# A hybrid attention layer on one core: new homes for the rotary tables, the dilated mask, the far values and the probability tiles

## The reference

```
h = x @ w_in + b_in                      # 1024 x 3072: qa ka va | qb kb vb | qc | z
oa = banded attention, window 128, 8 query heads on 2 key heads, rotary, learned sinks
ob = dilated attention, 4 heads, rotary: key distances <= 128 (step 1), <= 512 (step 4),
     <= 2048 (step 16), merged by their softmax denominators
oc = attention of 4 heads to keys and values from mem @ w_mem
y  = concat(rms(oa), rms(ob), rms(oc)) * g_branch * silu(z)
x  = layer_norm(2 ** 0.25 * x + y @ w_out)
```

## Time and profile before

| what | value |
|---|---|
| median of three runs | 519.87 us |
| span of the profiled execution, first to last instruction | 512.1 us |
| the profiled execution's own time from outside | not listed; the median lies 7.8 us above the span |
| PE (TensorE matmul) busy | 487.5 us, 95% |
| DVE / ACT / POOL busy | 328.4 / 214.9 / 72.7 us |
| mean granted TensorE clock | 0.992 |

### The profile page before, as it was taken

How to read it: one execution, slowest core, us unless ns; L and a number is a source line. 1 busy time by engine, 2 the same in 40 slices (tenths; PEclk the granted TensorE clock), 3 DMA queues, 4 the chain that set the end, 5 groups by cost and what they waited for, 6 DMA issues and landing times.

```text
span 512.1 us, 9694 instructions
## 1 busy us (share of the span) xinstructions
PE 487.5 (95%) x3480; PEld 443.9 (87%) x3480; DVE 328.4 (64%) x908; ACT 214.9 (42%) x488; POOL 72.7 (14%) x53
## 2 busy tenths in 40 slices
PE   4999999999999979999999898999989999999993
PEld 4999999999999968888888787898878788888882
DVE  4776645557666723444444568878797969798734
ACT  5632222021212035555463659655444454444530
POOL 0000000000000000111101101023232323231425
PEclk9999999999999989999999999999999999999998
DMA  8955472647622453321322179324232414241022
GB/s 288 375 194 146 126 236 82 206 140 257 217 89 93 142 147 105 102 86 56 107 85 91 54 234 316 99 63 135 71 127 60 149 53 148 63 142 48 1 83 82
DMA packets 51710, 67.83 MB, mean 132 GB/s; under 512 B 9552, under 2 KB 41296, under 8 KB 51664
## 3 DMA queue, kind: packets, MB, share of 16 engines
q1 hardware_dynamic: 51088, 66.17, 40.4%
q10 hardware_dynamic: 576, 1.05, 0.6%
HBM read 51.18 MB, written 16.02 MB: 131 GB/s over the span
## 4 chain that ended last, share of the span: by engine, by line
PE 88%; DVE 7%; ACT 2%; DMA 1%; issue 1%; POOLq 0%; POOL 0%; SPq 0%; ACTq 0%; DVEq 0%
PE long_ps L948 15%; PE o_ps L907 9%; PE wide L770 8%; PE wide L772 7%; PE wide L771 7%; PE long_ps L849 5%; PE long_ps L847 5%; PE long_ps L848 5%; PE narrow L887 4%; PE wide L875 4%; PE wide L876 3%; PE wide L781 2%; PE wide L782 2%; PE wide L783 2%; PE narrow L925 1%; DVE nb L1349 1%
## 5 line engine op out<-in xcount | busy, mean ns | idle before, releaser
L770 PE MATMUL wide<-x_hi,w_hi 128*128 128x256 f32 x320 | 88.5, 277 | 0.2
L771 PE MATMUL wide<-x_lo,w_hi 128*128 128x256 f32 x320 | 88.3, 276 | 0.0
L772 PE MATMUL wide<-x_hi,w_lo 128*128 128x256 f32 x320 | 88.3, 276 | 0.0
L770 PEld LDWEIGHTS wide<-x_hi,w_hi 128*128 128x128 f32 x320 | 60.1, 188 | 0.5 <-issue 0.5
L771 PEld LDWEIGHTS wide<-x_lo,w_hi 128*128 128x128 f32 x320 | 60.1, 188 | 0.0
L772 PEld LDWEIGHTS wide<-x_hi,w_lo 128*128 128x128 f32 x320 | 60.1, 188 | 0.0
L1029 ACT ACTIVATE spill<-turn 128x512 fp32r<-128x512 f32 x21 | 13.3, 633 | 99.3 <-DVE turn L1261 73.2
L948 PE MATMUL long_ps<-wo_hi,y_hi 128*128 128x512 f32 x128 | 53.1, 415 | 0.0
L1510 POOL TENSOR_TENSOR g_lo<-g_raw,g_hi 128x1024 fp32r<-128x1024 f32 x6 | 14.3, 2385 | 273.1 <-ACT g_hi L1034 273.1
L948 PE MATMUL long_ps<-wo_lo,y_hi 128*128 128x512 f32 x128 | 52.3, 408 | 0.0
L948 PE MATMUL long_ps<-wo_hi,y_lo 128*128 128x512 f32 x128 | 51.7, 404 | 0.0
(11 more groups left out here) (154 smaller groups left out, 1208.9 us busy)
## 6 DMA issues: line engine op xcount, KB each, us to landing
q_spill<-spill SPq DMA_DIRECT2D x32, 256.0 KB, 2.5
q_pair<-q_spill SPq DMA_DIRECT2D x128, 64.0 KB, 2.0
w_raw<-in_w_qkv SPq DMA_DIRECT2D x12, 512.0 KB, 5.7
x_raw<-in_x_t SPq DMA_DIRECT2D x16, 256.0 KB, 7.7
g_raw<-in_w_gate SPq DMA_DIRECT2D x8, 512.0 KB, 3.5
q_pair<-q_spill SPq DMA_DIRECT2D x32, 128.0 KB, 2.7
q_pair<-q_spill SPq DMA_DIRECT2D x128, 32.0 KB, 1.8
wo_raw<-in_w_out SPq DMA_DIRECT2D x8, 512.0 KB, 4.7
```

Source lines behind the costliest of these rows:

```text
L770: pe.matmul(dst, w_hi[s][:, k, f], t_hi[:, k, cols], start=(k == 0), stop=False)
L771: pe.matmul(dst, w_hi[s][:, k, f], t_lo[:, k, cols], start=False, stop=False)
L772: mm = pe.matmul(dst, w_lo[s][:, k, f], t_hi[:, k, cols], start=False, stop=(k == KT - 1))
```

## The change

- `cos_t` and `sin_t` now lie in the bytes of `v_far`. Nothing shares with `mask_b` any more.
- `mask_b` is loaded among the first loads, behind `sides`.
- The eight `v_far` loads move from jobs 5 to 8 into SP's attention loop, two in each of v = 6, 7, 8, 9.
- `prob[0]` and `prob[1]` trade bytes (21 turned jobs is odd), so `prob[0]` lies on `spill[1]` and `prob[1]` on `spill[0]`.
- ACT waits ahead of the loop for the store of m = 19 only. DVE waits for no store ahead of the loop; it waits for both at unit 1, its first write into a `prob` tile.

```
+FAR_VALUES_AT = 6
...
-        v_far = at("v_far", [P, 2, CLASSES, HB, VW], F32, Region(nbytes(2, CLASSES, HB, VW)).base)
+        r_v = Region(nbytes(2, CLASSES, HB, VW))
+        v_far = at("v_far", [P, 2, CLASSES, HB, VW], F32, r_v.base)
+        cos_t = at("cos_t", [P, SEQ], F32, r_v.base)
+        sin_t = at("sin_t", [P, SEQ], F32, r_v.base + nbytes(SEQ))
...
-        prob = [at(f"prob{s}", [P, SEQ], F32, r_t.base + s * nbytes(SEQ)) for s in range(2)]
+        n_turned = len(plan.turned)
+        prob = [at(f"prob{s}", [P, SEQ], F32, r_t.base + (n_turned + s) % 2 * nbytes(SEQ)) for s in range(2)]
...
-        cos_t = at("cos_t", [P, SEQ], F32, r_p.base)
...
-        r_m = Region(nbytes(SEQ))
-        mask_b = at("mask_b", [P, SEQ], F32, r_m.base)
-        sin_t = at("sin_t", [P, SEQ], F32, r_m.base)
+        mask_b = at("mask_b", [P, SEQ], F32, Region(nbytes(SEQ)).base)
...
             sp.dma_start(sides[:, :, :], sides_d).then_inc(mask_a_in, 16)
+            sp.dma_start(mask_b[:, :], mask_b_d).then_inc(mask_b_in, 16)
...
-                if 5 <= n < 5 + CLASSES:
-                    load_far_values(n - 5)
...
             sp.wait_ge(h_read, n_jobs)
-            sp.dma_start(mask_b[:, :], mask_b_d).then_inc(mask_b_in, 16)
...
                     load_queries(v + QS - 1)
+                if FAR_VALUES_AT <= v < FAR_VALUES_AT + CLASSES:
+                    load_far_values(v - FAR_VALUES_AT)
...
-            for n in plan.turned[-2:]:
-                act.wait_ge(*spills(n))
+            act.wait_ge(*spills(plan.turned[-2]))
...
                     dve.wait_ge(mask_b_in, 16)
+                    for n in plan.turned[-2:]:
+                        dve.wait_ge(*spills(n))
...
             dve.wait_ge(mask_a_in, 48)
-            for n in plan.turned[-2:]:
-                dve.wait_ge(*spills(n))
```

More of the change, by code:

```diff
@@ L398, in layer @@
         v_c = at("v_c", [P, NBM, HC, VW], F32, Region(nbytes(NBM, HC, VW)).base)
-        v_far = at("v_far", [P, 2, CLASSES, HB, VW], F32, Region(nbytes(2, CLASSES, HB, VW)).base)
+        r_v = Region(nbytes(2, CLASSES, HB, VW))
+        v_far = at("v_far", [P, 2, CLASSES, HB, VW], F32, r_v.base)
+        cos_t = at("cos_t", [P, SEQ], F32, r_v.base)
+        sin_t = at("sin_t", [P, SEQ], F32, r_v.base + nbytes(SEQ))
+        assert r_v.base + nbytes(2, SEQ) <= r_v.end
         r_z = Region(nbytes(FT, SEQ))
```

## The result

Forecast 515.1 us, range 514.3 to 517.2. Measured in the first comparison: **513.44 us** (median of four executions, 510.77 to 513.83) against 519.93 us for the kernel before (four executions, 519.07 to 521.63), a ratio of 0.9864 [0.9834, 0.9894]. The direction was right; the time lies 0.9 us under the range. The ratios leave out executions on record as slow (over 1.5% above the fastest of the same kernel), and in the 5th set these are three of the changed kernel's six, so that 0.9835 rests on three. The two medians of that set, 514.22 and 518.74 us, differ by 0.9%. The kernel before has 90 executions in the later sets of runs, with a median of 519.5 us (514.6 to 523.6); its four of the first comparison have no clock on record and are left out of the 90.

A forecast was written before the change was run, and what follows sets the result against it. TensorE was taken as the bound (88% of the 512.1 us span), so only its idle or slow-clock stretches counted. Terms 3.14 + 1.67 = 4.81 us off 519.87 gave 515.1 us, range 514.3 to 517.2.

The forecast's parts named there:

- Term 1: Start of attention: the wait for the last store moves behind unit 0, so TensorE's transposes begin 3.14 us earlier.
- Term 2: Gate matmuls behind that idle, from 186 us: without the idle the clock does not fall, 1.67 us gained.
- The rule set against this term: Start of attention: very short, frequent idles can swing the clock; then term 2 is 0, sum 3.14 us; rival's chance 0.07.
- The mask as a condition: Unit 1's exponential: with a late mask TensorE would stand over 4 us; early load itself earns 0.
- The far loads and the tables' home at zero: Far loads moved from projection to attention iterations 6 to 9 cost 0; the tables' new home changes no instruction.
- What is late next: At unit 2's scores, 186.2 us: its queries in time by 0.3 to 0.8 us, unit 1's probabilities by 0.4.
- the three runs before spread over 0.9 us: Whole kernel: step that widened the forecast's own range, 514.9 to 515.4, to 514.3 to 516.0 us.
- the median of the runs lies 7.8 us above that span: Whole kernel: the same distance was kept from span to time, giving 519.87 - 4.81 = 515.1 us.
- a span near 507.3 us: Whole kernel: sign that the prediction is right, the span of 512.1 us less 4.81 us.

The follow-up runs named there:

- homes only: Changed kernel with the old probability tiles and store waits put back, keeping new table homes, early mask and moved far loads: 518.40 us, 0.9974 to the kernel before.

## Why the prediction was wrong: its steps and its range

**Term 1, the wait for the store: right.** 3.27 us of idle became 0.10; forecast 0.13. The run without the trade left 2.38 us and cost 2.2 us more than the change. The rest of the span, without the clock's cost, fell by 3.15 us in the 3rd set of runs.

**Term 2, the clock: right on average, wrong in its bounds.** The split of the span into the clock's cost and the rest, over the 90 and the 28 executions, has means of 4.84 and 512.45 us before, 3.15 and 508.97 changed. The clock gave 4.84 − 3.15 = 1.69 us (± 0.4; forecast 1.67) and the rest 3.48 us (± 0.7; 3.0 by the medians, 512.48 − 509.47; forecast 3.14). But 1.67 stood there as an upper bound, read from a single profile, and it is none: behind the same length of idle the loss was 0, 1.6 and 2.7 us, and the fall near 315 us, which the prediction did not know of, comes and goes in both kernels. The earlier trace rows were read as an idle of 1.31 us with a full clock behind it. By the timeline of before that idle is 1.39 us, as the stretch ended just before it did:

```profile
294.08 0.50 PE L822 MATMUL long_ps<-x_hi,g_hi 128*128 128x512 f32 x1 [1.39 <-DVE zt L1342]
```

It is there in all fourteen profiles (1.38 or 1.39 us), each time with a full clock behind. Yet at 314 us a full clock followed an idle of 1.31 us, and a fall one of 1.00. So the row was right for its own place and no rule for another, and one profile cannot carry a bound.

The rule set against this term is from the Trainium skill, page "TensorE: Matmul & The Clock Gate", section "A second HAM failure mode: psum-queue depth-cycling": short but frequent idles between groups of matmuls can make the clock swing as well. At the start of the attention the trace does not show it: 1.00 from 186 to 190 us. At the output weights, where two waits come close together, the trace of the 3rd set of runs fits it (0.94 and 0.72), and three of the five profiles of the changed kernel do not, at 1.00. That fall is in one of two profiles of before and in two of five of the changed kernel, too few to tell whether it has a share in the difference of 1.69 us.

**The mask as a condition: right,** and 4.15 us of stall where it is not met. **The far loads and the tables' home at zero: right** as far as can be told. The ratio of homes only, 0.9974, lies inside the interval that before gives against itself, though its own [0.9950, 0.9999] leaves room for 2.6 us; PE has no idle in iterations 6 to 9.

**What is late next: right.** Unit 2's queries were in time, by less than forecast. Their landing in the changed kernel:

```profile
DMA to landing us min/median/max: 2.0/2.2/2.5
```

The last of the four loads was issued at 187.7 us, so all had landed by 190.2, 0.2 us before the scores at 190.38 (forecast: 0.3 to 0.8). Unit 1's exponential ended at 189.75, 0.6 us before unit 2's scores (forecast: 0.4).

**The step that failed** is the range, by two of its terms. The first is term 2's upper bound, "Bounds 0 (it falls all the same) and 1.67": one profile's loss was taken for the most that the clock can give back, and the next profile of the same kernel lost 2.7 us. Put into the prediction's own range, the 2.72 − 1.67 = 1.05 us more would have moved its low end from 514.3 to 513.25, and 513.44 would lie inside. The second is "the three runs before spread over 0.9 us, so 514.3 to 516.0". The spread of three executions was taken for that of the kernel. Over 90, before scatters from 514.6 to 523.6 us, and the changed kernel over 28 from 507.1 to 516.5. The range also allowed only 0.6 us on either side for the spread of 0.9, without a reason, and 519.87 − 2.9 − 1.67 is 515.3, not 515.4.

The measured 513.44 is in part the draw of the executions. The four of the changed kernel in the first comparison all had a clock of 0.995 or 0.996, a loss of 2.3 us where its mean is 3.15. That accounts for 0.8 us of the 1.0 by which 513.44 lies below the median of all 28. The first comparison's gain of 6.5 us was not seen again: the medians of the four later sets of runs differ by 4.7, 4.2, 4.8 and 4.5 us, where 4.81 was forecast. The median of all 28, 514.4, is just inside the range; of the four later sets two are inside (514.87, 515.59) and two less than 0.1 us below it (514.23, 514.22). By the ratio, the forecast was 515.1 / 519.87 = 0.9908, and the means of all executions give 514.06 / 519.22 = 0.9901. What the clocks of before were in the first comparison is not on record, so its share in the 6.5 us stays open.

A second step was false without harm: "the median of the runs lies 7.8 us above that span; with the same distance". The distance of an execution's time from its own span is 1.9 to 2.0 us; the rest was the quick projection of the profiled execution and a loss of clock smaller than the mean. The sign that it named, a span near 507.3 us, failed for this reason (511.6). As the idle is the same in either pace (3.27 and 3.24 us), the sum was not touched by it.

**Open:** why the projection runs at two paces (91 or 87 to 88 matmuls in ten microseconds at the same granted clock); why the same idle is followed by no fall, a short or a long one; whether the clock term is all from the start of the attention; and why executions at the same clock, 0.996, still differ by up to 3.8 us (514.53 and 510.77 us, changed kernel).

## What to carry to other kernels

A wait that stands ahead of a loop is often there for a reader deep inside it: find which unit really touches the storage, and let the unit that comes first use the storage that comes free first. But follow the queue one unit further before taking the credit, for here the same change without the early mask moved the stall by one unit and earned nothing. And a single profile gives sizes for one execution: before bounds are drawn from it, set its span beside the median, and if they differ by more than an execution's time differs from its own span (1.9 to 2.0 us here), the profiled execution is not a typical one.

## What was unexpected in the hardware

- The same idle of 3.2 us, between the same instructions, had three clock losses behind it: 0, 1.6 and 2.7 us (homes only, first profile of before, second profile of before).
- At one and the same place of one kernel the clock fell behind idles of 1.00 and 1.38 us (0.71 and 0.72 from 315 to 320 us) and stayed full behind 1.03, 1.12 and 1.31 us. Some 20 us earlier an idle of 1.38 or 1.39 us had a full clock behind it in all fourteen profiles.
- At a granted clock of 1.00 and with PE busy 10.00 of 10.00 us, the same code passed 91 matmuls in one profile and 87 or 88 in all thirteen others, which made 4 us and more by the start of the attention. The granted clock and the busy share together do not say how fast PE works.
